# Gated linear attention in a two-block transformer kernel: values' products of two chunks in one, an empty state left out, keys masked by ScalarE, a low-rank gate on four column groups

## Chip, cores and metric

One NeuronCore of a Trainium2 chip runs the whole kernel. The metric is the device time of one execution in microseconds (us), as the median over runs. Everything is float32.

## What is computed

Two blocks over 256 tokens of width 1024. The first block has two layers. Layer 0 mixes tokens with a delta rule and a sparse attention; layer 1 mixes them with gated linear attention (the "second mixer", which the change touches); each layer ends in a mixture of 32 experts. The second block (two more layers) is not touched. The second mixer, cut to what matters:

```python
def gla_mixer(h, w_in, w_gate2, b_gate2, out_norm, w_out):
    q, k, v, r, glr = split_cols(h @ w_in, [512, 512, 1024, 1024, 16])
    log_a = log_sigmoid(glr @ w_gate2 + b_gate2) / 16          # low-rank gate, rank 16
    o = gla_chunked(heads(q), heads(k), heads(v), heads(log_a))  # 4 heads, chunks of 64 tokens
    o = rms_norm(o, out_norm) * silu(heads(r))
    return o @ w_out

def step(state, xs):                       # one chunk of one head; state starts as zeros
    q_i, k_i, v_i, b_i = xs                # b_i: running sum of log_a in the chunk
    bl = b_i[-1:]
    o_inter = (q_i * exp(b_i)) @ state
    att = causal(sum_d q_i k_i exp(b_i - b_j))
    o = o_inter + att @ v_i
    state = state * exp(bl).T + (k_i * exp(bl - b_i)).T @ v_i
    return state, o
```

## The kernel before

All engines' programs are written out by hand and meet at semaphores (`q.e.wait_ge`, `.then_inc`); each engine runs its own list in order. Weights come through a ring of six slots of 2 MB in SBUF. SyncE (SP) issues one transfer per slot, in a fixed order, and waits only for `unit_done`, the count of pieces of work ("units") with which TensorE has let go of a slot (line 337 outside the experts, line 355 in their loop). PSUM has eight banks of 512 floats per partition.

The second mixer on TensorE is `pe_gla`, in this order:

- `pe_gla_in`: as soon as the normalised input arrives (eight pieces, ScalarE line 494), line 1480 makes the 16 gate features from eight products of 128x16 weights with 256 tokens. Then two slots of query and key features (helper `pe_features`, line 432), with the gate's second product (line 1489) between them, and two slots of values (helper `accumulate`, line 400). Queries and keys are laid out by feature, values by token.
- `pe_gla_att`: for two token tiles (t) and four heads, the 64x64 products inside each chunk (line 1584) into bank 0, and the transposes of the decayed keys (line 1587) into banks 1 and 2.
- VectorE (`dve_gla_att`) then masks: for each of the two chunks of a tile (par) the scores (line 1594) and the keys (line 1595, the other chunk's tokens made zero), and clears the state `gS` (line 1596). Only then it signals `att_read`, for which TensorE waits.
- `pe_gla_scan`, for each of four chunks: the keys' product with the values, which is what is added to the state (line 1608); the state's product with the decayed queries (line 1614) and the values' product with the masked scores (line 1615), eight each, 64 columns wide, one pair for each half of a head's output; and then one "fill", eight products of the output gate `r` (`pe_gla_fill`, line 400), under which VectorE forms the next state (line 1626).
- `pe_gla_out`: sums of squares per head (line 1391), more fills, and `pe_out`, the product with `w_out` (line 696), followed by the router and the experts of layer 1 (lines 1920, 1944, 1953, 1967, 1902).

A float32 product is two instructions in the trace (two MATMUL and two LDWEIGHTS), so the x-counts of lines 1480, 1489, 1608, 1614 and 1615 are twice the number of products; the transposes are one instruction each.

Of the kernel before, what the change touches and what calls it, by code (L numbers as in the profile page):

```python
# [19 lines left out]
P = 128  # L20
D = 1024
KD = D // P
S = 256
# [103 lines left out]
def parameter_columns(a):  # L127
# [10 lines left out]
    c["gdn_norm"] = cols(a["gdn_out_norm"][0])  # L138
    c["gla_w2"] = pad(np.asarray(a["gla_w_gate2"][0]))
    c["gla_b2"] = cols(a["gla_b_gate2"][0])  # L140
# [56 lines left out]
dve_step act_step  # L197
inputs_in constants_in moment_ready glr_ready x_ready scaled_ready unit_done lin_read silu_c ada_copied ada_columns ada_read
sq_ready sum_ready rstd_ready norm_ready root_ready var_ready
# [17 lines left out]
def build(nc, a, vec_at, vec_w, dense_at, out):  # L217

    ctx = ExitStack()
    with ctx:  # L220
# [1247 lines left out]
        eq, ek, eb, ed = (view(A0 + 9472 + 1024 * j, H, S) for j in range(4))  # L1468
        att = view(A0 + 13568, 2, TH, CH)
        gkd = view(A0 + 14592, 2, TH, P)  # L1470
# [4 lines left out]
        def pe_gla_in(q):  # L1475
            u = Units(q)
            s = slot(q)
            for k in range(KD):
                q.e.wait_ge(sems["norm_ready"], q.due("norm_ready"))
                ins = mm(psum[0:16, 5, 0:S], narrow(s, 16)[:, k, :], hT[:, k, :], start=(k == 0), stop=(k == KD - 1))  # L1480
            ins.then_inc(sems["unit_done"], 1)
            for j in range(2):
                s = slot(q)
                for n in range(2):
                    pe_features(u, s, hT, 2 * P * n)
                if j == 0:
                    q.e.wait_ge(sems["glr_ready"], q.due("glr_ready"))
                    for h in range(H):
                        ins = mm(banks(6, 2, H, S)[:, h, :], v("gla_w2")[0:16, P * h:P * h + P], glr[0:16, :], start=True, stop=True)
                    ins.then_inc(sems["cums_ready"], 1)  # L1490
            for j in range(2):
                s = slot(q)
                for t in range(NT):
                    pe_tokens(u, s, hT, 0, 512, t)
            u.end()

        def act_gla_in(q):
            q.e.wait_ge(sems["unit_done"], q.due("unit_done"))
            A.activation(glr[0:16, :], psum[0:16, 5, 0:S], ACT.Copy).then_inc(sems["glr_ready"], 1)
            for j in range(2):  # L1500
# [75 lines left out]
        def pe_gla_att(q):  # L1576
# [11 lines left out]
            ins.then_inc(sems["att_ready"], 1)  # L1588

        def dve_gla_att(q):  # L1590
            q.e.wait_ge(sems["att_ready"], q.due("att_ready"))
            half = v("half", 2, CH)
            for par in range(2):
                V.tensor_tensor(att[:, par], banks(0, 1, TH, CH), over(half[:, par, :], TH), ALU.mult)
                V.tensor_scalar(gkd[:, par], banks(1, 2, TH, P), v("par")[:, par:par + 1], None, ALU.mult)
            V.memset(gS, 0.0).then_inc(sems["att_read"], 1)
            q.e.wait_ge(sems["att_read"], q.due("att_read"))

        def pe_gla_scan(q):

            q.e.wait_ge(sems["att_read"], q.due("att_read"))
            outs = banks(4, 4, 2 * H, S)
            for c in range(NCH):
                t, par = c // 2, c % 2
                if c > 0:
                    q.e.wait_ge(sems["state_ready"], q.due("state_ready"))
                for h in range(H):
                    ins = mm(psum[:, 2 + h // 2, S * (h % 2):S * (h % 2) + S], gkd[:, par, t * H + h, :], gv[:, t, S * h:S * h + S],
                             start=True, stop=True)
                ins.then_inc(sems["dstate_ready"], 1)  # L1610
                for h in range(H):
                    for i in range(2):
                        o = outs[:, 2 * h + i, CH * c:CH * c + CH]
                        mm(o, gS[:, h, P * i:P * i + P], eb[:, h, CH * c:CH * c + CH], start=True, stop=False, skip_group_check=True)
                        ins = mm(o, gv[:, t, S * h + P * i:S * h + P * i + P], att[:, par, t * H + h, :], start=False, stop=True,
                                 skip_group_check=True)
                ins.then_inc(sems["scan_out"], 1)
                pe_gla_fill(q, c)
            pe_gla_fill(q, NCH)

        def dve_gla_scan(q):
            for c in range(NCH - 1):
                q.e.wait_ge(sems["dstate_ready"], q.due("dstate_ready"))
                q.e.wait_ge(sems["scan_out"], q.due("scan_out"))
                for h in range(H):
                    ins = V.scalar_tensor_tensor(out=gS[:, h, :], in0=gS[:, h, :], scalar=ebl[:, NCH * h + c:NCH * h + c + 1],
                                                 in1=psum[:, 2 + h // 2, S * (h % 2):S * (h % 2) + S], op0=ALU.mult, op1=ALU.add)
                ins.then_inc(sems["state_ready"], 1)
            q.skip("dstate_ready")
            q.skip("scan_out")  # L1630
# [50 lines left out]
        def act_gla(q):  # L1681
            act_gla_in(q)
            act_gla_out(q)
            q.skip("unit_done", 4)
# [1290 lines left out]
```

## Time and profile before

| what | value |
|---|---|
| median of 3 runs | 2617.33 us (2615.58 to 2617.4) |
| the profiled execution's own time | 2615.79 us |
| its span | 2614.0 us |
| mean granted TensorE clock | 0.985 of full |
| second mixer, from its first product to its last product of `w_out`'s stage | 808.8 to about 966 us of the span |

The rows further down come from the profiled execution. Times in them are from the start of its span. PE is TensorE's matrix products, PEld its weight loads, DVE is VectorE, ACT is ScalarE, SPq is SyncE's queue. A granted clock of 1.00 is 2.4 GHz and 0.50 is 1.2 GHz.

### The profile page before, as it was taken

To read this page: it belongs to the slowest core of one execution; us is meant where nothing else is said; L and a number is where in the kernel's file an instruction comes from. 1 tells how busy PE (TensorE), PEld (TensorE's weight loads), DVE (VectorE), ACT (ScalarE), POOL (GpSimd) and SP (SyncE) were. 2 spreads that over 40 slices of the span, in tenths; PEclk is the share of its full clock that TensorE was granted. 3 is DMA by queue.
4 is the path that set the end of the run, shared out by engine and by line. 5 is a ranking of instruction groups with operands and counts; after the bars stand their busy time and mean duration, and the time that the engine had idled before them with its cause. 6 is when DMAs were issued, how large, how long until landed. Compare 5 with 4: busy or idle time off the path is not lost.

```text
span 2614.0 us, 28378 instructions
## 1 busy us (share of the span) xinstructions
PE 2441.6 (93%) x11488; PEld 1398.9 (54%) x11488; DVE 676.6 (26%) x1400; ACT 450.1 (17%) x814; POOL 0.2 (0%) x4
## 2 busy tenths in 40 slices
PE   7999999888889999988888999999999999999998
PEld 5775743333336673333333777774444777874443
DVE  3653321111003232101001533134112533042113
ACT  3141110000002121000000133102111242112111
POOL 0000000000000000000000000000000000000000
PEclk9999999999999999999999899999999999999999
DMA  9348669999997138999999532246999232148994
GB/s 402 132 188 366 250 282 428 428 429 428 428 427 289 73 129 335 429 428 428 429 428 427 215 129 97 97 192 239 425 422 416 110 129 97 65 193 331 426 421 187
DMA packets 53941, 769.64 MB, mean 294 GB/s; under 512 B 5984, under 2 KB 6496, under 8 KB 7008
## 3 DMA queue, kind: packets, MB, share of 16 engines
q1 hardware_dynamic: 53568, 768.17, 71.2%
q8 instruction: 62, 1.02, 0.1%
q10 hardware_dynamic: 288, 0.26, 0.1%
q14 instruction: 23, 0.19, 0.0%
HBM read 767.36 MB, written 1.05 MB: 294 GB/s over the span
## 4 chain that ended last, share of the span: by engine, by line
PE 71%; DMA 23%; DVE 3%; ACT 2%; issue 1%; SPq 0%; ACTq 0%; DVEq 0%
DMA slab<-in_experts 22%; PE psum L400 14%; PE psum L432 13%; PE psum L1930 8%; PE psum L1920 8%; PE psum L1967 7%; PE psum L1902 6%; PE psum L696 4%; PE psum L503 1%; DMA slab<-in_dense 1%; PE psum L1240 1%; PE psum L1953 1%; PE psum L626 0%; PE psum L1944 0%; PE psum L746 0%
## 5 line engine op out<-in xcount | busy, mean ns | idle before, releaser
L1920 PE MATMUL psum<-slab 128*64 128x512 f32 x2048 | 461.1, 597 | 77.6 <-DMA slab<-in_experts 73.8
L400 PE MATMUL psum<-slab 128*128 128x256 f32 (+6 forms) x1560 | 389.1, 406 | 12.2 <-ACT slab L2480 7.0
L1967 PE MATMUL psum<-slab 128*64 128x512 f32 x1536 | 359.5, 603 | 2.6 <-ACT slab L1998 2.6
L432 PE MATMUL psum<-slab 128*128 128x256 f32 x1504 | 345.4, 391 | 11.8 <-DVE slab L2770 6.6
L1920 PEld LDWEIGHTS psum<-slab 128*64 128x64 f32 x2048 | 142.1, 137 | 390.3 <-issue 274.7
L400 PEld LDWEIGHTS psum<-slab 128*128 128x128 f32 (+2 forms) x1560 | 272.9, 188 | 121.6 <-issue 70.6
L432 PEld LDWEIGHTS psum<-slab 128*128 128x128 f32 x1504 | 294.1, 196 | 60.9 <-issue 8.8
L1902 PE MATMUL psum<-slab 128*128 128x256 f32 x1024 | 249.3, 385 | 1.2 <-DVE slab L2020 1.2
L1930 PE MATMUL psum<-slab 128*64 128x512 f32 x1024 | 225.3, 592 | 0.0
L1902 PEld LDWEIGHTS psum<-slab 128*128 128x128 f32 x1024 | 183.2, 189 | 72.7 <-issue 50.3
L2010 DVE TENSOR_TENSOR slab<-psum,slab 128x512 f32<-128x512 f32 (+1 forms) x64 | 35.7, 558 | 691.6 <-PE psum L1920 502.3
L1967 PEld LDWEIGHTS psum<-slab 128*64 128x64 f32 x1536 | 99.3, 137 | 182.1 <-issue 178.5
L1930 PEld LDWEIGHTS psum<-slab 128*64 128x64 f32 x1024 | 73.4, 137 | 145.3 <-issue 145.0
L1994 ACT ACTIVATE slab<-psum 128x512 f32<-128x512 f32 (+1 forms) x64 | 31.4, 491 | 600.8 <-PE psum L1920 346.8
L696 PE MATMUL psum<-slab 128*128 128x256 f32 x512 | 114.8, 381 | 0.0
L696 PEld LDWEIGHTS psum<-slab 128*128 128x128 f32 x512 | 95.9, 189 | 17.0 <-issue 3.7
L2020 DVE COPY slab<-psum 128x256 f32<-128x256 f32 x64 | 27.2, 425 | 287.7 <-PE psum L1953 287.7
L1998 ACT ACTIVATE slab<-psum 128x512 f32<-128x512 f32 (+1 forms) x64 | 31.4, 491 | 387.0 <-PE psum L1944 387.0
L2026 DVE COPY slab<-psum 128x512 f32<-128x512 f32 x64 | 44.3, 692 | 147.0 <-PE psum L1967 147.0
L2002 ACT ACTIVATE slab<-psum 128x512 f32<-128x512 f32 x64 | 38.2, 597 | 198.6 <-PE psum L1967 198.6
L447 ACT ACTIVATE slab<-psum 128x512 f32<-128x512 f32 (+3 forms) x45 | 25.4, 565 | 243.3 <-PE psum L432 173.5
L2768 DVE TENSOR_TENSOR slab<-psum,slab 128x1024 f32<-128x1024 f32 x16 | 19.6, 1225 | 182.9 <-PE psum L400 182.9
(429 smaller groups left out, 1565.0 us busy)
## 6 DMA issues: line engine op xcount, KB each, us to landing
slab<-in_experts SPq DMA_DIRECT2D x288, 2048.0 KB, 20.2
slab<-in_dense SPq DMA_DIRECT2D x73, 2048.0 KB, 9.2
slab<-in_dense SPq DMA_DIRECT2D x2, 1680.0 KB, 16.8
slab<-in_vec SPq DMA_DIRECT2D x1, 2571.5 KB, 33.0
slab<-in_dense SPq DMA_DIRECT2D x1, 1328.0 KB, 27.6
slab<-in_dense SPq DMA_DIRECT2D x2, 640.0 KB, 13.9
slab<-in_xT SPq DMA_DIRECT2D x1, 1024.0 KB, 8.4
out<-slab SPq DMA_DIRECT2D x2, 512.0 KB, 2.6
```

The costliest lines, as they stand in the source:

```text
L400: ins = mm(out_ap, lhs, rhs, start=(n == 0), stop=(n == len(pairs) - 1), skip_group_check=True)
L432: ins = mm(psum[:, b, S * j:S * j + S], narrow(s, width)[:, k, c0 + P * j:c0 + P * j + P], src[:, k, :], start=(k == 0), stop=(k == KD - 1 ...
L696: ins = mm(psum[:, b, S * j:S * j + S], sl(w[n // 2], KD)[:, k, c0:c0 + P], src[:, k, :], start=(part is early and j == 0 and k == early[0 ...
L1902: ins = mm(y[:, c, :], ysl[:, P * c:P * c + P], gatedT, start=begin and c % 2 == 0, stop=False, skip_group_check=True)
L1920: ins = mm(psum[CAP * e:CAP * e + CAP, n, :], xg[:, k, CAP * e:CAP * e + CAP], sl(w, KD)[:, e * (KD // 2) + i, :], start=(k == 0), stop=(k ...
L1930: ins = mm(psum[CAP * e:CAP * e + CAP, 0, :], xg[:, k, CAP * e:CAP * e + CAP], sl(w[e], KD)[:, k, :], start=(k == 0), stop=(k == KD - 1), ...
L1967: ins = mm(psum[CAP * e:CAP * e + CAP, 2 + half, :], hidT[:, f, CAP * e:CAP * e + CAP], w, start=(f == 0), stop=(f == fc - 1), skip_group_ ...
L1994: A.activation(sil[:, 0:f], psum[:, 0, 0:f], ACT.Silu).then_inc(sems["silu_ready"], 1)
L1998: A.activation(hidT[:, 0:f // P, :], banks(0, 1, f // P, P), ACT.Copy).then_inc(sems["hidT_ready"], 1)
L2002: A.activation(ysl[:, 0:512], psum[:, 2, :], ACT.Copy).then_inc(sems["half_ready"], 1)
L2010: V.tensor_tensor(hid[:, 0:f], up, sil[:, 0:f], ALU.mult).then_inc(sems["hid_ready"], 1)
L2026: V.tensor_copy(ysl[:, 512:], psum[:, 3, :]).then_inc(sems["results_ready"], 1)
```

## The change

Five edits in the second mixer:

1. The gate features are made on four groups of 32 columns of TensorE: product k writes partitions 32(k mod 4) to 32(k mod 4)+31 of bank 5. The 128 rows then hold four partial sums, and the second product runs over all 128 rows, with `w_gate2` (16 rows, padded with zeros to 32) repeated four times, so that it adds them up.
2. The keys are masked by ScalarE (`act_gla_keys`, four activations of 512 columns with a scale per partition) while VectorE masks the scores alone, a tile at a time, with a signal after each tile.
3. The masked scores of a tile's two chunks stand beside each other, so that the values' product is made once for each tile, 128 columns wide.
4. Chunk 0 has no product with the empty state, the last chunk has no product of keys and values (nothing reads its state), and the state is not cleared: its first value is a copy.
5. Order in the scan: the values' products of tile 0 wait only for the first mask signal and run before the keys' products; the first fill waits for the second.

```diff
-    c["gla_w2"] = pad(np.asarray(a["gla_w_gate2"][0]))
+    c["gla_w2"] = np.concatenate([pad(np.asarray(a["gla_w_gate2"][0]))[:32]] * 4)
...
-        att = view(A0 + 13568, 2, TH, CH)
+        att = view(A0 + 13568, TH, P)
...
-                ins = mm(psum[0:16, 5, 0:S], narrow(s, 16)[:, k, :], hT[:, k, :], start=(k == 0), stop=(k == KD - 1))
+                g = k % 4
+                ins = mm(psum[32 * g:32 * g + 32, 5, 0:S], sl(s, KD)[:, 0, 16 * k:16 * k + 32], hT[:, k, :], start=(k < 4), stop=(k >= 4),
+                         skip_group_check=True)
...
-                        ins = mm(banks(6, 2, H, S)[:, h, :], v("gla_w2")[0:16, P * h:P * h + P], glr[0:16, :], start=True, stop=True)
+                        ins = mm(banks(6, 2, H, S)[:, h, :], v("gla_w2")[:, P * h:P * h + P], glr, start=True, stop=True)
...
-            A.activation(glr[0:16, :], psum[0:16, 5, 0:S], ACT.Copy).then_inc(sems["glr_ready"], 1)
+            A.activation(glr, psum[:, 5, 0:S], ACT.Copy).then_inc(sems["gla_copied"], 1)
...
+        def act_gla_keys(q):
+            q.e.wait_ge(sems["att_ready"], q.due("att_ready"))
+            for t in range(NT):
+                for par in range(2):
+                    ins = A.activation(gkd[:, par, t * H:t * H + H, :], banks(1 + t, 1, H, P), ACT.Copy, scale=v("par")[:, par:par + 1])
+            ins.then_inc(sems["gla_copied"], 1)
...
-            for par in range(2):
-                V.tensor_tensor(att[:, par], banks(0, 1, TH, CH), over(half[:, par, :], TH), ALU.mult)
-                V.tensor_scalar(gkd[:, par], banks(1, 2, TH, P), v("par")[:, par:par + 1], None, ALU.mult)
-            V.memset(gS, 0.0).then_inc(sems["att_read"], 1)
-            q.e.wait_ge(sems["att_read"], q.due("att_read"))
+            for t in range(NT):
+                own = slice(t * H, t * H + H)
+                for par in range(2):
+                    ins = V.tensor_tensor(att[:, own, CH * par:CH * par + CH], banks(0, 1, TH, CH)[:, own, :], over(half[:, par, :], H), ALU.mult)
+                ins.then_inc(sems["att_read"], 1)
...
-            q.e.wait_ge(sems["att_read"], q.due("att_read"))
             outs = banks(4, 4, 2 * H, S)
             for c in range(NCH):
                 t, par = c // 2, c % 2
+                if c == 0:
+                    q.e.wait_ge(sems["att_read"], q.due("att_read"))
+                if par == 0:
+                    for h in range(H):
+                        for i in range(2):
+                            ins = mm(outs[:, 2 * h + i, P * t:P * t + P], gv[:, t, S * h + P * i:S * h + P * i + P], att[:, t * H + h, :],
+                                     start=(c == 0 and i == 0), stop=False, skip_group_check=True)
+                if c == 0:
+                    ins.then_inc(sems["scan_out"], 1)
+                    q.e.wait_ge(sems["gla_copied"], q.due("gla_copied"))
+                else:
+                    q.e.wait_ge(sems["state_ready"], q.due("state_ready"))
+                if c < NCH - 1:
+                    for h in range(H):
+                        ins = mm(psum[:, 2 + h // 2, S * (h % 2):S * (h % 2) + S], gkd[:, par, t * H + h, :], gv[:, t, S * h:S * h + S],
+                                 start=True, stop=True)
+                    ins.then_inc(sems["dstate_ready"], 1)
                 if c > 0:
-                    q.e.wait_ge(sems["state_ready"], q.due("state_ready"))
-                for h in range(H):
-                    ins = mm(psum[:, 2 + h // 2, S * (h % 2):S * (h % 2) + S], gkd[:, par, t * H + h, :], gv[:, t, S * h:S * h + S],
-                             start=True, stop=True)
-                ins.then_inc(sems["dstate_ready"], 1)
-                for h in range(H):
-                    for i in range(2):
-                        o = outs[:, 2 * h + i, CH * c:CH * c + CH]
-                        mm(o, gS[:, h, P * i:P * i + P], eb[:, h, CH * c:CH * c + CH], start=True, stop=False, skip_group_check=True)
-                        ins = mm(o, gv[:, t, S * h + P * i:S * h + P * i + P], att[:, par, t * H + h, :], start=False, stop=True,
-                                 skip_group_check=True)
-                ins.then_inc(sems["scan_out"], 1)
+                    for h in range(H):
+                        for i in range(2):
+                            ins = mm(outs[:, 2 * h + i, CH * c:CH * c + CH], gS[:, h, P * i:P * i + P], eb[:, h, CH * c:CH * c + CH],
+                                     start=False, stop=(par == 1), skip_group_check=True)
+                    ins.then_inc(sems["scan_out"], 1)
+                if c == 0:
+                    q.e.wait_ge(sems["att_read"], q.due("att_read"))
                 pe_gla_fill(q, c)
             pe_gla_fill(q, NCH)
...
-                q.e.wait_ge(sems["scan_out"], q.due("scan_out"))
-                for h in range(H):
-                    ins = V.scalar_tensor_tensor(out=gS[:, h, :], in0=gS[:, h, :], scalar=ebl[:, NCH * h + c:NCH * h + c + 1],
-                                                 in1=psum[:, 2 + h // 2, S * (h % 2):S * (h % 2) + S], op0=ALU.mult, op1=ALU.add)
-                ins.then_inc(sems["state_ready"], 1)
-            q.skip("dstate_ready")
+                if c == 0:
+                    q.skip("scan_out")
+                    V.tensor_copy(gS, banks(2, 2, H, S)).then_inc(sems["state_ready"], 1)
+                    q.e.wait_ge(sems["state_ready"], q.due("state_ready"))
+                else:
+                    q.e.wait_ge(sems["scan_out"], q.due("scan_out"))
+                    for h in range(H):
+                        ins = V.scalar_tensor_tensor(out=gS[:, h, :], in0=gS[:, h, :], scalar=ebl[:, NCH * h + c:NCH * h + c + 1],
+                                                     in1=psum[:, 2 + h // 2, S * (h % 2):S * (h % 2) + S], op0=ALU.mult, op1=ALU.add)
+                    ins.then_inc(sems["state_ready"], 1)
+                    q.e.wait_ge(sems["state_ready"], q.due("state_ready"))
             q.skip("scan_out")
...
         def act_gla(q):
             act_gla_in(q)
+            act_gla_keys(q)
             act_gla_out(q)
```

## Rows read from the trace of the kernel before

**Rows 1.** The page's chain that ended last, share of the span by engine.

```profile
PE 71%; DMA 23%; DVE 3%; ACT 2%; issue 1%; SPq 0%; ACTq 0%; DVEq 0%
```

**Rows 2.** The DMA queue's waits, 790 to 1200: us in total, times, longest us.

```profile
SPq L355 <- PE psum L1920: 117.5, 32, 16.4
SPq L337 <- PE psum L400: 88.3, 4, 45.1
```

**Rows 3.** Windows by stage: busy us of PE, PEld, DVE, ACT, POOL; clock, DMA share, GB/s.

```profile
808.70:814.05 5.35, 5.24 (x16) 1.87 (x16) 2.17 (x6) 2.76 (x7) 0.00 (x0) 0.68 1.00 423
1100.00:1500.00 400.00, 357.73 (x1613) 161.28 (x1612) 71.89 (x161) 35.13 (x58) 0.00 (x0) 0.98 0.94 396
```

**Rows 4.** Timeline of the mixer's first stage: start us, us, engine, line.

```profile
808.16 3.30 ACT L494 ACTIVATE slab<-slab 128x256 f32<-128x256 f32 x8 [1.59 <-DVE slab L2142]
808.82 5.31 PE L1480 MATMUL psum<-slab 128*16 128x256 f32 x16 [1.27 <-ACT slab L494]
810.69 0.15 PEld L1480 LDWEIGHTS psum<-slab 128*16 128x16 f32 x1 [0.28 <-ACT slab L494]
811.12 0.15 PEld L1480 LDWEIGHTS psum<-slab 128*16 128x16 f32 x1 [0.28 <-issue]
814.05 14.14 PE L432 MATMUL psum<-slab 128*128 128x256 f32 x64
```

**Rows 5.** Timeline: 32-column groups after a full product, and what follows them.

```profile
920.44 1.08 PE L1391 MATMUL psum<-slab 128*32 128x256 f32 x16
921.44 3.74 PE L400 MATMUL psum<-slab 128*128 128x256 f32 x16
```

**Rows 6.** Timeline from the scores to the scan's first product.

```profile
873.41 1.09 PE L1587 MATMUL psum<-slab 128*128 128x128 f32 x8
874.54 0.69 DVE L1594 TENSOR_TENSOR slab<-psum,slab 128x512 f32<-128x512 f32 x1 [12.74 <-PE psum L1587]
878.38 0.91 DVE L1596 MEMSET slab<- 128x1024 f32 x1 [0.16 <-issue]
879.34 3.78 PE L1608 MATMUL psum<-slab 128*128 128x256 f32 x8 [4.83 <-DVE slab L1596]
```

**Rows 7.** Windows of 0.5 us at the clock's steps, columns as in rows 3.

```profile
812.50:813.00 0.50, 0.50 (x4) 0.23 (x3) 0.00 (x0) 0.00 (x0) 0.00 (x0) 1.00 1.07 459
877.50:878.00 0.50, 0.00 (x0) 0.00 (x0) 0.50 (x1) 0.00 (x0) 0.00 (x0) 0.50 1.05 426
884.50:885.00 0.50, 0.50 (x7) 0.50 (x6) 0.00 (x0) 0.00 (x0) 0.00 (x0) 1.00 0.00 0
```

**Rows 8.** Timeline of the scan: chunk 1 from its keys' product, and chunk 3's end.

```profile
882.92 0.52 PE L1614 MATMUL psum<-slab 128*128 128x64 f32 x2
887.03 3.69 PE L400 MATMUL psum<-slab 128*128 128x256 f32 x16
890.56 1.90 PE L1608 MATMUL psum<-slab 128*128 128x256 f32 x8
892.29 0.33 PE L1614 MATMUL psum<-slab 128*128 128x64 f32 x2
895.81 3.69 PE L400 MATMUL psum<-slab 128*128 128x256 f32 x16
896.08 1.66 DVE L1626 SCALAR_TENSOR_TENSOR slab<-slab,psum 128x256 f32<-128x256 f32 x4 [7.08 <-PE psum L1615]
913.35 7.16 PE L400 MATMUL psum<-slab 128*128 128x256 f32 x32
```

**Rows 9.** Timeline: products 128 columns wide with 128x128 weights.

```profile
974.55 3.84 PE L400 MATMUL psum<-slab 128*128 128x128 f32 x32 [0.84 <-DVE slab L1798]
```

**Rows 10.** Timeline: ScalarE's four activations with operands per partition, 512 columns.

```profile
969.31 2.79 ACT L678 ACTIVATE slab<-psum,slab 128x512 f32<-128x512 f32 x4 [0.23 <-DVE slab L657]
```

**Rows 11.** Groups of VectorE by form: busy us, mean ns, idle before.

```profile
L2010 DVE TENSOR_TENSOR slab<-psum,slab 128x256 f32<-128x256 f32 x32 | 13.6, 424 | 189.3 <-ACT slab L1994 189.3
L2694 DVE COPY slab<-psum 128x1024 f32<-128x1024 f32 x2 | 2.4, 1224 | 19.1 <-PE psum L2676 19.1
```

More of the change, by code:

```diff
@@ L197 @@
 dve_step act_step
-inputs_in constants_in moment_ready glr_ready x_ready scaled_ready unit_done lin_read silu_c ada_copied ada_columns ada_read
+inputs_in constants_in moment_ready gla_copied x_ready scaled_ready unit_done lin_read silu_c ada_copied ada_columns ada_read
 sq_ready sum_ready rstd_ready norm_ready root_ready var_ready
@@ L1486, in pe_gla_in @@
                 if j == 0:
-                    q.e.wait_ge(sems["glr_ready"], q.due("glr_ready"))
+                    q.e.wait_ge(sems["gla_copied"], q.due("gla_copied"))
                     for h in range(H):
-                        ins = mm(banks(6, 2, H, S)[:, h, :], v("gla_w2")[0:16, P * h:P * h + P], glr[0:16, :], start=True, stop=True)
+                        ins = mm(banks(6, 2, H, S)[:, h, :], v("gla_w2")[:, P * h:P * h + P], glr, start=True, stop=True)
                     ins.then_inc(sems["cums_ready"], 1)
@@ new lines, in pe_gla_scan @@
+                if c == 0:
+                    ins.then_inc(sems["scan_out"], 1)
+                    q.e.wait_ge(sems["gla_copied"], q.due("gla_copied"))
+                else:
[5 more added lines that the diff above has]
+                    ins.then_inc(sems["dstate_ready"], 1)
```

## The prediction

> **What bounds the kernel now.** I read the chain that ended last first: 71% of it is TensorE and 23% transfers, VectorE and ScalarE have 5% between them [rows 1]. So a microsecond counts where TensorE is the one that is waited for, and for the transfers one must ask what starts them. The DMA queue's waits answer that: in the experts' loop (line 355) and outside it (line 337) SyncE waits for TensorE's units, and for nothing that runs by a clock of its own [rows 2]. In the experts of layer 1 the transfers are the pace (DMA share 0.94, TensorE 358 of 400 us busy, not 400) [rows 3], but their stream begins when the first slots are let go, which is when the mixer has ended. So whatever the mixer loses or gains on TensorE moves the start of that stream, and all that comes later, by the same amount: I take the factor as 1. In the mixer's first stage the transfers are at 1.00 of their time [rows 3], but TensorE passes from the gate features into the next slot's work without a gap [rows 4], so the weights were there.
>
> Inside the mixer the timeline shows TensorE as the chain nearly throughout, with one real hole: from the end of the transposes to the scan it waits 4.83 us for VectorE's masks [rows 6]. The windows show two stretches at half the granted clock (1.2 GHz): one before 812.5 us in the first stage, whose mean clock is 0.68 [rows 3, 7], and one from about 877 us, in that hole, to about 884 us [rows 7].
>
> **Term 1, gate features on column groups.** Before: the 16 instructions of line 1480 start at 808.82 and line 432 follows at 814.05. The inputs came earlier: ScalarE's eighth piece ends at 808.16 + 3.30 = 811.46. What made the end late is that at 1.2 GHz one instruction takes 0.43 us (811.12 - 810.69) while a piece needs two and arrives every 0.41 [rows 4]. On four groups products of different groups overlap: the sixteen 32-column instructions of line 1391 take 921.44 - 920.44 = 1.00 us, against the 3.5 us that sixteen full ones of the same length take (887.03 to 890.56) [rows 5, 8]. Then TensorE keeps up, and only the last piece's own two instructions lie behind its arrival: 811.46 + 0.05 for the signal (879.34 after VectorE's 878.38 + 0.91 [rows 6]) + 2 x 0.43, and 0.1 for the change back to full width (four rounds of 0.215 are 0.86, and line 1391 took 1.00), is 812.45. Gain 814.05 - 812.45 = 1.6. Bounds: 1.9 if the clock were back by then; 0.2 if it had never been low, since at 0.215 us an instruction the old order keeps up with the pieces too. I take 1.6, for nothing ahead of it changes. Wider weights (32 columns for 16), the second product over 128 rows for 16 and the copy over 128 partitions cost nothing: eight instructions of 256 columns take 1.90 with all 128 rows too [rows 8], and the copy has those 14 us of line 432's work over it [rows 4].
>
> **Term 2, the masks.** Before: transposes end, VectorE starts at 874.54, runs 4.8 us, TensorE starts at 879.34 [rows 6]. After: VectorE's first signal comes after two TENSOR_TENSORs of 256 columns at 0.42 [rows 11], overlapping a little: 0.8 us. TensorE starts at 875.4. Gain 3.95. The second signal is due 0.8 later and is wanted only by the first fill, 3.5 us later; nothing stands there. ScalarE's four activations start at 874.54 too. The nearest row has two operands per partition and takes 2.79 for four [rows 10]; the new ones have one, so 2.4 to 2.8, ready at 876.9 to 877.4. ScalarE had nothing to do then (its next work is the first fill's output), and it reads banks 1 and 2, VectorE bank 0. TensorE wants the keys when the values' products of tile 0 are done, at 875.4 + 1.8 = 877.2. Stall 0 to 0.25; I take 0.1. If ScalarE were twice as slow, 2.8.
>
> **Term 3, fewer products.** Sixteen products (eight with the state, eight with the values) take 895.81 - 892.29 = 3.52 us, 0.22 each, 0.11 an instruction [rows 8]. Now merge two chunks: is a 128-column product dearer than a 64-column one? Thirty-two instructions of just that form take 978.39 - 974.55, that is 3.84 us with their start, 0.12 each [rows 9]. The weight load sets both, so the merged product costs what one of the two did, and half of 32 are gone, and eight of 32 state products with chunk 0: 24 x 0.22 = 5.3. [...] Lower bound from the rows: 0.12 for 0.11, 0.3 us less. Chunk 3's keys' products: eight instructions, 892.29 - 890.56 = 1.73 [rows 8]. Nobody reads them. Gain 1.73. Together 7.0.
>
> **Term 4, the state.** VectorE forms the state under a fill: 1.66 us, begun 0.27 after the fill begins, against 3.5 of fill [rows 8]. The first state is now a copy of 1024 columns, 1.22 [rows 11], begun after the keys' products, also under the fill. Cost 0 with 1.6 us to spare; without the fill it would be 1.9 for a state and 1.5 for the copy. The clearing (0.91) was in the hole of term 2 and is counted there.
>
> **Term 5, the clock in the scan.** The low stretch begins in the hole and ends in chunk 0. Chunk 0's keys' products took 882.92 - 879.34 = 3.58 against 1.73, its sixteen others 887.03 - 882.92 = 4.11 against 3.52 [rows 6, 8]: 1.85 + 0.59 = 2.4. With the hole down to 0.9 us I expect the clock to stay at 2.4 GHz. Gain 2.4; bounds 0 (it falls all the same) and 2.4.
>
> **The rest.** Everything from the last state products on (squares, two fills, roots, `w_out`) keeps its order and its distances. Check by a walk, in the old times: 875.4, tile 0's values 1.8, stall 0.1, keys 1.73, fill 3.5: 882.5; chunk 1 1.73 + 1.76 + 3.5: 889.5; chunk 2 8.8: 898.3; chunk 3 1.76: 900.1. Before, the fills after chunk 3 begin at 913.35 [rows 8]. That is 13.2, and 1.6 of term 1 makes **14.8 us**.
>
> **How the numbers follow.** The profiled execution took 2615.79; 2615.79 - 14.8 = 2601.0. The median of the runs is 1.5 us higher, so the median after should be 2617.33 - 14.8 = **2602.5**. The bound of no change is 0.2%, 5.2 us, for all that follows.
>
> **Rivals.**
> - *The clock falls after all.* TensorE still pauses for 0.9 us after the transposes. Against it: it fell some 3 us into a hole of 4.83 us [rows 6, 7], and this one is over sooner. Price 1.7 to 2.4: 2604.2 to 2604.9. 12%. The Trainium skill (TensorE: Matmul & The Clock Gate, Part 4) holds that transposes don't count as work for the clock gate, which would make this likelier; no row here separates them.
> - *The column groups give nothing*, because the pieces are the pace or the low stretch lies elsewhere: term 1 is 0.2, 2603.9. 6%.
> - *A 128-column product costs two.* 3.5 back: 2606.0. Against it rows 9. 6%.
> - *The gain doesn't reach the end*, because the experts' transfers run on a schedule that the mixer doesn't set: 2617. Against it, every wait of SyncE is for TensorE [rows 2]. 5%.
> - *Slower: TensorE stays at 1.2 GHz through the scan.* Its products are now mostly short ones behind weight loads; if those don't bring the clock up, the 24.7 us of work from 875.4 to 900.1 take 49.4. That gives back 24.7 of 14.8, and ends 9.9 above before: 2627.2. Half of the low time is lost, so it decides from 29.6 us at the low level. Against it: the clock rose at 884 us in the middle of just such products [rows 7]. 2%.
> - The forecast itself: 69%.
>
> Faster by over 0.2% in the first three rivals and the forecast: 0.93. Same 0.05, slower 0.02. Range: the forecast's own terms run from 14.2 to 15.5 (2601.8 to 2603.1); the three small rivals reach 2606.0; the runs of before spread over 1.8 us. So 2600.0 to 2606.5.
>
> **What would show it.** Line 1480's last product ends about 1 us after ScalarE's last piece. TensorE's hole before the scan is under 1 us and the granted clock there 1.00. The values' products, 32 instructions in two runs of 16, take 1.8 us a run. No stall over 0.3 before the first keys' products; none before the state's. Seven fills as before. The experts' first transfers shift by 14 to 15 us. The prediction is wrong if the stretch from the last norm piece to `w_out` is not 14 to 15 us shorter, or if it is and the end isn't.

## The result, and the profile after

| | before | changed |
|---|---|---|
| median | 2615.31 us (6 runs, 2612.49 to 2617.4) | 2600.06 us (6 runs, 2599.09 to 2604.06) |
| profiled execution, its own time | 2615.79 us | 2600.23 us |
| its span | 2614.0 us | 2598.6 us |

The ratio is 0.994 with an interval of 0.9928 to 0.9952, a gain of 15.3 us between the medians. In a second comparison on another occasion (5 and 9 runs) it was 0.9941 (0.9928 to 0.9955). The forecast was a gain of 14.8 us and a median of 2602.5.

The page's chain by engine is the same line as in [rows 1], and SyncE still waits for TensorE only. Its first transfer in the experts' loop (line 355) is issued at 968.90 where it was 982.17, 13.3 us sooner, in an execution whose mixer began 2.2 us later. Its longest wait outside that loop was 45.1 us and is 31.6 now, because the units it waits for in the scan come sooner (the waits of [rows 2]):

```profile
SPq L337 <- PE psum L400: 74.9, 4, 31.6
```

The first stage, from the timeline (the counterpart of [rows 4]); line 1481 is the gate features' product now, line 1491 the gate's second product:

```profile
810.37 3.31 ACT L494 ACTIVATE slab<-slab 128x256 f32<-128x256 f32 x8 [1.59 <-DVE slab L2168]
811.02 3.67 PE L1481 MATMUL psum<-slab 128*32 128x256 f32 x16 [1.27 <-ACT slab L494]
814.62 14.13 PE L432 MATMUL psum<-slab 128*128 128x256 f32 x64
828.59 1.89 PE L1491 MATMUL psum<-slab 128*128 128x256 f32 x8
830.32 14.03 PE L432 MATMUL psum<-slab 128*128 128x256 f32 x64
844.18 27.63 PE L400 MATMUL psum<-slab 128*128 128x512 f32 x64
```

TensorE now follows ScalarE's pieces: they end at 813.68, and line 432 starts 0.94 later (before, 2.59 later). First gate product to line 432 is 3.60 us, before 5.23. The same part of the timeline before, from the gate's second product (line 1489) on:

```profile
828.12 1.99 PE L1489 MATMUL psum<-slab 16*128 16x256 f32 x8
844.01 27.63 PE L400 MATMUL psum<-slab 128*128 128x512 f32 x64
```

From the first query and key product to the first values' product (line 400) it was 844.01 - 814.05 = 29.96 us and is 844.18 - 814.62 = 29.56 now. The windows show that the gate features of the changed kernel were made at 1.2 GHz too (columns as in [rows 3]):

```profile
811.00:814.62 3.62, 3.60 (x17) 1.42 (x17) 2.08 (x6) 2.68 (x7) 0.00 (x0) 0.53 1.02 430
814.62:816.00 1.38, 1.38 (x7) 1.24 (x7) 0.00 (x0) 0.38 (x1) 0.00 (x0) 1.00 1.10 427
```

From the scores to the scan and through it (the counterpart of [rows 6] and [rows 8]); line 1586 is the scores, 1605 VectorE's masks, 1596 ScalarE's, 1618 the values' products, 1627 the keys', 1633 the state's, 1646 the copy of the first state, 1651 the later states:

```profile
873.58 1.09 PE L1589 MATMUL psum<-slab 128*128 128x128 f32 x8
874.71 1.42 DVE L1605 TENSOR_TENSOR slab<-psum,slab 128x256 f32<-128x256 f32 x4 [12.74 <-PE psum L1589]
874.71 2.42 ACT L1596 ACTIVATE slab<-psum,slab 128x512 f32<-128x512 f32 x4 [2.27 <-PE psum L1589]
875.52 2.05 PE L1618 MATMUL psum<-slab 128*128 128x128 f32 x16 [0.85 <-DVE slab L1605]
877.41 1.90 PE L1627 MATMUL psum<-slab 128*128 128x256 f32 x8
879.15 3.63 PE L400 MATMUL psum<-slab 128*128 128x256 f32 x16
879.35 1.22 DVE L1646 COPY slab<-psum 128x1024 f32<-128x1024 f32 x1 [3.22 <-PE psum L1627]
882.61 1.90 PE L1627 MATMUL psum<-slab 128*128 128x256 f32 x8
884.35 1.89 PE L1633 MATMUL psum<-slab 128*128 128x64 f32 x16
886.08 3.69 PE L400 MATMUL psum<-slab 128*128 128x256 f32 x16
...
900.11 7.15 PE L400 MATMUL psum<-slab 128*128 128x256 f32 x32
```

The hole before the scan is 0.85 us where it was 4.83. ScalarE is done at 877.13, VectorE with all scores at 876.13, and TensorE comes for the keys at 877.3: no stall worth naming. Every later product begins where the one before it ends. And the clock stayed up from the scores to the scan's end:

```profile
873.00:901.00 28.00, 27.15 (x188) 24.78 (x183) 5.95 (x13) 4.99 (x7) 0.00 (x0) 1.00 0.18 71
```

**The walk.** The figure that I follow through the experiments is the *stretch*, from the first product of the gate features to the first product with `w_out` (line 696), both read from the timeline; what is left of the span is the *rest*, in which all kernels here but the last two have the same code.

| kernel | stretch begins | stretch | rest |
|---|---|---|---|
| before | 808.8 | 124.9 | 2489.1 |
| changed | 811.0 | 109.4 | 2489.2 |
| changed, once more | 810.7 | 109.7 | 2489.4 |
| old gate chain | 814.1 | 111.5 | 2493.9 |
| before, column groups alone | 812.4 | 122.4 | 2487.5 |
| gate chain at full width | 808.4 | 110.9 | 2488.6 |
| values' products 64 wide | 808.5 | 113.0 | 2481.1 |
| keys masked by VectorE | 810.1 | 110.7 | 2487.3 |
| all masks first | 809.5 | 113.8 | 2485.9 |
| hole filled with products | 810.0 | 113.2 | 2486.1 |
| hole filled with transposes | 811.4 | 112.5 | 2490.0 |
| scores early | 808.3 | 107.6 | 2488.6 |
| scores early, fillers at layer 0's end | 808.5 | 107.2 | 2485.3 |
| scores early, fillers at four ends | 808.7 | 107.2 | 2484.8 |

The stretch lost 15.5 us and the rest nothing (2489.1, 2489.2). That these two rests agree so closely is in part luck, for the rests of the other kernels, with the same code there, lie between 2481.1 and 2493.9. That what the mixer gained reaches the end whole rests on the medians: 15.3 us here and 16.1 in the second comparison, for 15.5 in the stretch.

### The profile page after: what moved, and what is told of

It is laid out like the page before. It is cut to its first block, busy times and chain, and to the rows that moved or that the text cites. A ratio compares the mean times of both kernels' runs of the same rounds, so it can differ in the third digit from the quotient of the medians.

```text
span 2598.6 us, 28266 instructions
## 1 busy us (share of the span) xinstructions
PE 2428.8 (93%) x11432; PEld 1390.5 (54%) x11432; DVE 672.8 (26%) x1396; ACT 452.2 (17%) x818; POOL 0.2 (0%) x4
## 4 chain that ended last, share of the span: by engine, by line
PE 71%; DMA 23%; DVE 3%; ACT 2%; issue 1%; SPq 0%; ACTq 0%; DVEq 0%
DMA slab<-in_experts 22%; PE psum L400 14%; PE psum L432 13%; PE psum L1956 8%; PE psum L1946 8%; PE psum L1993 7%; PE psum L1928 6%; PE psum L696 4%; PE psum L503 1%; DMA slab<-in_dense 1%; PE psum L1240 1%; PE psum L1979 1%; PE psum L626 0%; PE psum L1970 0%; PE psum L746 0%
```

## The experiments

**Old gate chain.** The changed kernel with the first edit undone.

```diff
-                ins = mm(psum[32 * g:32 * g + 32, 5, 0:S], sl(s, KD)[:, 0, 16 * k:16 * k + 32], hT[:, k, :], start=(k < 4), stop=(k >= 4),
+                ins = mm(psum[0:16, 5, 0:S], narrow(s, 16)[:, k, :], hT[:, k, :], start=(k == 0), stop=(k == KD - 1))
...
+                        ins = mm(banks(6, 2, H, S)[:, h, :], v("gla_w2")[0:16, P * h:P * h + P], glr[0:16, :], start=True, stop=True)
```

> The changed kernel with the gate features made by the old chain of 16 columns. Measure: the stretch from the first gate-feature product to the first product with w_out, 109.4 us in the changed kernel, 124.9 in the one before. By terms: 1.6 of the chain comes back, and 0.3 for which the walk has no term yet, seen around the gate's second product (16 rows before, 128 after): 111.3. Rival, the column groups give only what the late clock gives: where the clock is at 2.4 GHz during the chain, the stretch stays within 0.5 us of 109.4.

Measured: stretch 111.5, 2607.05 us for one execution. The chain:

```profile
814.07 5.33 PE L1480 MATMUL psum<-slab 128*16 128x256 f32 x16 [1.28 <-ACT slab L494]
819.33 13.92 PE L432 MATMUL psum<-slab 128*128 128x256 f32 x63
```

5.26 us to line 432, not 3.60, and the distance between the two query and key slots 15.99, not 15.70; from the first of them to the values' products it is 29.96, not 29.56. The terms hold; the clock was low here, so the rival was not tried at its own condition.

**Column groups alone**, on the kernel before.

> The kernel before with the column groups alone. By terms: the stretch is 124.9 - 1.9 = 123.0, with the hole before the scan still 4.8 us long and the granted clock low from inside the hole into the first chunk. Rival: products that fill only 32 columns each don't bring the clock back as fast as the chain did, and the query products after them run at 1.2 GHz for some us: 124 or more.

Measured: stretch 122.4, 2611.57 us for one execution. The hole is still 4.84 us, as the timeline has it:

```profile
881.12 3.65 PE L1610 MATMUL psum<-slab 128*128 128x256 f32 x8 [4.84 <-DVE slab L1598]
```

The windows show that the clock fell only just behind it and was low for 3.4 us. In the profile of before it fell inside the hole and was still low for 4.8 us of work behind it [rows 7]:

```profile
881.40:884.50 3.10, 3.10 (x8) 2.42 (x8) 0.00 (x0) 0.00 (x0) 0.00 (x0) 0.50 0.00 0
884.80:886.00 1.20, 1.20 (x13) 1.20 (x13) 0.00 (x0) 0.00 (x0) 0.00 (x0) 1.00 0.00 0
```

From the keys' first product to the end of chunk 3 it is 33.35 us here and 34.01 before: 0.66 of the 2.4 gained against forecast is the place of the fall. With it put back the stretch is 123.1 for 123.0 expected. In this execution the clock was low until 816.4, 0.35 us into the query products, and the rival's price, 124 or more, did not come. Among all profiles here in which the clock was low over the gate features, it rose 2.6 to 4.8 us after their first product with the groups, and 3.3 to 3.7 us after it with the three chains. So whether the groups ever delay it is not settled.

**Gate chain at full width**: 128 columns of weights, of which 16 count; the others meet rows of zeros.

```diff
+                ins = mm(psum[:, 5, 0:S], sl(s, KD)[:, 0, 16 * k:16 * k + 128], hT[:, k, :], start=(k == 0), stop=(k == KD - 1))
```

> The changed kernel with one chain of full width (128 columns of weights, of which 16 are the gate's, the others meet rows of zeros in the second product) and the second product over 128 rows. If the 0.3 us at the second product comes from its 16 rows, this kernel keeps that gain and loses only the overlap of groups: 109.4 + 1.6 = 111.0, and the distance from the first to the second slot of query and key products is 15.7, not 16.0. Rival, the 0.3 belongs to the column groups: 111.3 and 16.0.

The timeline (line 1480 the gate features, 1489 the second product):

```profile
808.44 5.32 PE L1480 MATMUL psum<-slab 128*128 128x256 f32 x16 [1.27 <-ACT slab L494]
813.59 14.03 PE L432 MATMUL psum<-slab 128*128 128x256 f32 x64
827.46 1.89 PE L1489 MATMUL psum<-slab 128*128 128x256 f32 x8
829.18 14.03 PE L432 MATMUL psum<-slab 128*128 128x256 f32 x64
```

Measured: stretch 110.9, 2601.18 us for one execution; first gate product to line 432 5.15, and 15.59 between the slots. So the gain at the second product doesn't belong to the column groups: it comes from its 128 rows, with which there is no step between row widths on either side of it. This kernel is another 0.1 below the changed one's 15.70 because it has no step back from narrow weights either: its first slot takes 13.87 us, behind the groups it takes 13.97.

**Values' products 64 wide.**

```diff
-                            ins = mm(outs[:, 2 * h + i, P * t:P * t + P], gv[...], att[:, t * H + h, :], ...)
+                            for x in range(2):
+                                ins = mm(outs[:, 2 * h + i, P * t + CH * x:P * t + CH * x + CH], gv[...],
+                                         att[:, t * H + h, CH * x:CH * x + CH], ...)
```

> The changed kernel with each values' product of 128 columns split into two of 64 with the same weights. By terms a product of either width costs 0.22, so 16 more cost 3.5 us: the stretch is 112.9. Rival, a product's time goes by its columns: no change, 109.4.

The timeline of the values' products (line 1619) and the keys' (1629):

```profile
873.00 3.79 PE L1619 MATMUL psum<-slab 128*128 128x64 f32 x32 [0.85 <-DVE slab L1605]
876.62 1.96 PE L1629 MATMUL psum<-slab 128*128 128x256 f32 x8
```

Measured: 3.62 us for 32 instructions where the changed kernel has 1.89 for 16 of twice the width; stretch 113.0. An instruction of 64 or of 128 columns with its weight load costs 0.11 us. This execution took 2595.77 us, less than the changed kernel, with a stretch 3.6 longer: its rest was 8.1 shorter. One execution's total says nothing about a few microseconds here.

**Keys masked by VectorE**, after the scores, as before the change.

```diff
+            for par in range(2):
+                ins = V.tensor_scalar(gkd[:, par], banks(1, 2, TH, P), v("par")[:, par:par + 1], None, ALU.mult)
+            ins.then_inc(sems["gla_copied"], 1)
...
-            act_gla_keys(q)
```

> The changed kernel with the keys masked by VectorE, after the scores. TensorE still starts with the values' products 0.8 us after the transposes, but the keys are ready only after 1.4 + 2.5 us of VectorE, at 3.95 after the transposes, when the values' products have been done for 1.3 us: stretch 109.4 + 1.4 = 110.8, clock at 2.4 GHz throughout the scan. Rival, ScalarE's help is worth the whole of the old wait: 113 or more.

The timeline: values' products (line 1621), VectorE's masking of the keys (1608), keys' products (1630):

```profile
874.61 2.05 PE L1621 MATMUL psum<-slab 128*128 128x128 f32 x16 [0.85 <-DVE slab L1605]
875.13 2.46 DVE L1608 TENSOR_SCALAR slab<-psum,slab 128x1024 f32<-128x1024 f32 x2
877.65 2.00 PE L1630 MATMUL psum<-slab 128*128 128x256 f32 x8 [0.99 <-DVE slab L1608]
```

Measured: 3.04 us from the values' products to the keys', for 1.89, and stretch 110.7; 2600.69 us, ratio 0.9943 (0.9927 to 0.9958) beside 0.9941 for the changed kernel in the same comparison. ScalarE's part is worth 1.2 us; the rest of the hole went because the values' products no longer wait for the keys.

**All masks first**: the same, and the scan waits for them all.

```diff
                 if c == 0:
                     q.e.wait_ge(sems["att_read"], q.due("att_read"))
+                    q.e.wait_ge(sems["gla_copied"], q.due("gla_copied"))
```

> As e4, and the scan begins only when all masks are done: a hole of about 4 us before the scan, as before the change (4.8), with all other edits in. By terms: 3.1 us of the hole come back, and the clock falls inside it, which costs 1.7 to 2.4 more: stretch 114.2 to 114.9. Rival, the clock doesn't go by the hole: 112.5 with 2.4 GHz throughout. Total time between the two kernels, 5 us above the changed one.

The timeline, with the values' products in line 1622 and the keys' in 1630:

```profile
876.75 3.59 PE L1622 MATMUL psum<-slab 128*128 128x128 f32 x16 [3.98 <-DVE slab L1608]
880.13 2.01 PE L1630 MATMUL psum<-slab 128*128 128x256 f32 x8
```

The windows in the hole and after it:

```profile
873.00:876.50 3.50, 0.00 (x0) 0.00 (x0) 3.50 (x6) 0.00 (x0) 0.00 (x0) 1.00 1.02 435
877.00:880.00 3.00, 3.00 (x16) 3.00 (x16) 0.00 (x0) 0.00 (x0) 0.00 (x0) 0.50 0.02 5
```

Measured: stretch 113.8, 2604.31 us, ratio 0.9956 (0.9941 to 0.9971). The hole is 3.1 longer and the clock is low right behind it: the 16 values' instructions take 3.38 for 1.89. From the last transpose to `w_out` it is 50.76 us, 46.02 in the changed kernel: 3.13 of hole and 1.6 of clock. The clock was expected to fall inside the hole; it fell some 0.2 us behind its end and was low for 3.4 us of work. The stretch is 0.4 under the range expected (114.2 to 114.9): the clock cost a little less than 1.7, and in this execution the gate features took 3.25 us for 3.60, because the clock rose sooner there. The total was 3.5 above the changed kernel's, not 5. The hole itself is 0.85 shorter than before the change, with the clearing of the state gone from it.

**The hole filled.** The kernel just shown, with work in the hole that nothing reads: eight products of 256 columns, or 32 transposes.

```diff
+                    for _ in range(8):
+                        mm(psum[:, 3, 0:S], ident, v("gla_w2")[:, 0:S], start=True, stop=True)
```

> As the kernel in which the scan waits for all masks (hole 4.25 us from the last transpose to the scan's first product, clock low from inside it), with eight products of 256 columns into a free bank, 3.4 us of work that nothing reads, put into the hole. If the clock falls because TensorE stands still, it stays at 2.4 GHz here and the stretch is 113.8 - 1.6 = 112.2. Rival, the clock falls by something else in this place: again 113.8.

> The same, with 32 transposes (0.11 us each, 3.5 us) in the hole instead of the products. If transposes keep the clock up as products do, the stretch is 112.2 to 112.4. Rival, by which transposes don't count: the clock is low as in the kernel with the bare hole and the stretch 113.8 or, as more of it lies in the scan, up to 114.5.

The timeline with products in the hole (line 1618; 1624 the values', 1632 the keys'):

```profile
874.14 3.62 PE L1618 MATMUL psum<-slab 128*128 128x256 f32 x16
878.28 2.02 PE L1624 MATMUL psum<-slab 128*128 128x128 f32 x16 [0.52 <-DVE slab L1608]
880.14 1.90 PE L1632 MATMUL psum<-slab 128*128 128x256 f32 x8
```

The same with transposes in the hole (line 1618):

```profile
874.83 3.65 PE L1618 MATMUL psum<-slab 128*128 128x128 f32 x32
878.98 2.02 PE L1624 MATMUL psum<-slab 128*128 128x128 f32 x16 [0.49 <-DVE slab L1608]
```

The clock after the hole with transposes:

```profile
877.00:880.00 3.00, 2.51 (x23) 2.30 (x22) 1.83 (x2) 0.00 (x0) 0.00 (x0) 1.00 0.62 257
```

Measured: from the last transpose of the keys to `w_out` 49.12 and 49.14 us, for 50.76 with the bare hole. The scan begins just as late (4.25 us) and at 2.4 GHz. The clock fell in or just behind the hole in all three profiles with a bare hole of about 4 us and more, and in neither of these two, one execution each (2600.95 us with products, 2604.21 with transposes). So it is TensorE's standing still that brings the clock down, worth 1.6 us, and transposes hold it as well as products. The stretch was 112.5 with transposes, as expected, and 113.2 with products, a miss by 1: there the clock was low over the gate features for 6.8 us and into the query products (16.23 us between the slots for 15.70), ahead of the place in question.

**The changed kernel once more.**

> The changed kernel once more, unchanged, to see what moves between executions. By the walk the stretch from the first gate-feature product to the first w_out product is again 109.4 within 0.5, unless the clock's low stretch lies otherwise; outside it the two executions differ by several us at places where TensorE pauses, by where the granted clock falls. Rival, the difference between kernels outside the mixer (-7.6 and +5 us) belongs to the change: it is there again, at the same places.

Measured: 2600.78 us (2598.3 to 2602.47, 5 runs), stretch 109.7. The differences outside the mixer were partly there again and partly not. The windows over 1510 to 1660 us, first before (mean clock 0.97):

```profile
1510.00:1660.00 150.00, 139.43 (x644) 109.62 (x643) 53.05 (x53) 48.11 (x85) 0.00 (x0) 0.97 0.30 109
```

then the changed kernel (1.00):

```profile
1510.00:1660.00 150.00, 139.44 (x694) 116.12 (x692) 51.57 (x48) 46.67 (x86) 0.00 (x0) 1.00 0.30 107
```

and the changed kernel once more (0.97):

```profile
1510.00:1660.00 150.00, 139.44 (x671) 115.18 (x670) 51.53 (x48) 46.16 (x84) 0.00 (x0) 0.97 0.29 104
```

The same program has 1.00 in one execution and 0.97 in the next over 150 us. Over 2000 to 2250 us it is the other way round: 0.97 before, 0.95 in the changed kernel, 0.97 in the changed kernel once more. So a clock that falls at one layer's end and not at another's needs no change of the program; these places are not to be put down to the change.

**Scores early.** The hole and the pause ahead of the scores are both covered by the last piece of the values' products: scores, transposes and masks go ahead of it, and the wait for its copy goes behind the first values' products, which don't need it. The transposes wait until ScalarE has read bank 2 (`need`).

```diff
                 for t in range(NT):
+                    if j == 1 and t == 1:
+                        pe_gla_att(q, u)
                     pe_tokens(u, s, hT, 0, 512, t)
-            u.end()
...
+            u.need(u.n)
...
+                if n == 3:
+                    act_gla_keys(q)
...
                     q.e.wait_ge(sems["gla_copied"], q.due("gla_copied"))
+                    q.last_units.end()
```

> The changed kernel with the score products and transposes moved ahead of the last piece of the values' products, the keys' masking ahead of that piece's copy, and the wait for that copy behind the values' products of tile 0. Both pauses of TensorE (0.7 us before the scores, 0.85 before the scan) go: stretch 109.4 - 1.5 = 107.9, total 1.5 us below the changed kernel. Rival, the pauses move: the transposes wait for ScalarE to read bank 2 (up to 0.3), and what waits at the scan is the last copy: stretch 109 or more.

The timeline from the transposes (line 1594) over the last piece of values (400) to the scan (1623 the values' products, 1633 the keys'); ScalarE masks in line 1601:

```profile
863.30 1.09 PE L1594 MATMUL psum<-slab 128*128 128x128 f32 x8
864.23 7.03 PE L400 MATMUL psum<-slab 128*128 128x512 f32 x16
864.43 2.42 ACT L1601 ACTIVATE slab<-psum,slab 128x512 f32<-128x512 f32 x4 [1.51 <-PE psum L1594]
871.10 1.95 PE L1623 MATMUL psum<-slab 128*128 128x128 f32 x16
872.88 1.90 PE L1633 MATMUL psum<-slab 128*128 128x256 f32 x8
```

Measured: stretch 107.6, no pause left between 863 and the scan's end; 2597.13 us (5 runs, 2595.82 to 2597.91), ratio 0.9926 (0.9912 to 0.9939), against 2600.78 for the changed kernel in the same comparison. The slowest of its five executions is faster than the fastest of those five. The stretch is 0.3 shorter than expected: 1.76 from the two pauses, and the stall of 0.1 on the keys went too. The walk gives 1.8 us of the 3.7 between these two medians; the rest I can't tell from the spread.

**Fillers at layer 0's end.** On top of the scores early, products that nothing reads in the two pauses ahead of the gate features: five ahead of the wait for the statistics' scales, three after the products that spread them.

```diff
+            if m == 0:
+                for _ in range(5):
+                    mm(psum[:, 5, 0:S], ident, v("gla_w2")[:, 0:S], start=True, stop=True)
```

> The kernel with the scores early (stretch 107.6 us), with five and three products that nothing reads in the two pauses ahead of the gate features, where TensorE waits for the statistics and the first normalised piece. If the low stretch over the gate features comes from these pauses, the clock is 2.4 GHz there, and the last piece's two instructions take 0.43 instead of 0.86: 3.2 from the first gate product to the first query product instead of 3.6, stretch 107.1. Rival, the pauses are too long to be covered and the clock falls all the same: 107.6.

Windows over the pauses and the gate features, with the fillers:

```profile
803.50:808.50 5.00, 4.78 (x24) 3.71 (x25) 4.24 (x16) 0.93 (x3) 0.00 (x0) 1.00 1.00 423
808.50:812.00 3.50, 3.50 (x18) 1.32 (x18) 2.08 (x6) 2.79 (x8) 0.00 (x0) 1.00 1.01 431
```

and in the kernel with the scores early alone:

```profile
803.50:808.30 4.80, 1.29 (x8) 0.86 (x8) 4.03 (x15) 0.92 (x3) 0.00 (x0) 1.00 0.99 423
808.30:812.00 3.70, 3.67 (x17) 1.45 (x17) 2.09 (x6) 2.68 (x7) 0.00 (x0) 0.54 1.02 434
```

Measured: the clock is 1.00 over the gate features instead of 0.54, they take 3.24 us instead of 3.62, and the stretch is 107.2. In all twelve profiles without fillers the clock was low over the gate features, and in neither of the two with them. One execution, 2594.22 us.

**Fillers at four ends**, the same after each mixture of experts.

> The same fillers after each of the four expert mixtures, on top of the scores early. If the low stretches there are worth what half the clock costs, the total is 1 to 4 us below that of the scores early (2597.1 beside 2616.9), and the executions spread less. Rival, TensorE is not what is waited for in these places, or the fillers delay the rows' products: same total or 0.5 us more.

Measured: 2594.07 us (6 runs, 2592.39 to 2598.35), ratio 0.9918 (0.9902 to 0.9935), mean granted clock 0.991 where the scores early had 0.987. The median is 3.1 us below that of the scores early, which was taken in another comparison, and the two intervals overlap; that the fillers gain outside the mixer is likely and not shown. The executions spread over 6.0 us, more than the 2.1 of the scores early, so that part of the expectation was wrong.

## Where the prediction held, and the step that failed

The mechanisms of the five terms came as forecast, and the median lies inside the range, by 0.06 us. By its own sign the prediction failed: it called itself wrong if the stretch was not 14 to 15 us shorter, and the stretch is 15.5 shorter. The step that failed is a term put at nothing. Of "the second product over 128 rows for 16" the prediction says that it costs nothing; it counted no gain for it, and the change of rows gained 0.4 us.

*Term 1, 1.6 us.* Measured 5.23 - 3.60 = 1.63. The overlap is what it rests on: full width without groups gave 5.15. The allowance of 0.1 for the step back to full width holds where the clock is 1.00 (fillers at layer 0's end): line 432 starts 0.60 us behind the last piece there, of which the signal and two instructions are 0.48. In the changed kernel it was 0.94 for 1.01 expected, with the clock rising in the last 0.2 us. (The prediction's own sum gives 812.47 and not 812.45.) That the same is worth only 0.2 at 2.4 GHz was not tried.

*The term that was missing, 0.4.* I compared the second product over 128 rows with a product over 128 rows elsewhere (1.90 us), and never asked what the 16 rows of before had cost. From the first query and key product to the values' products it is 29.96 us before and with the old chain, and 29.56 in the changed kernel. The 0.4 lie in the second product (1.92 to 1.73 from start to start), in the slot ahead of it (0.1) and in the slot behind it (0.1). The 128 rows cost nothing, as the prediction said; what it missed is that the 16 rows had cost something, at the change of rows on both sides of the old product.

*Term 2, 3.95.* Measured 4.83 - 0.85 = 3.98. Of this 0.85 is the clearing of the state, which is gone (the hole is 3.98 with all masks first); 2.0 is the order, values before keys; and 1.2 is ScalarE's help, as the kernel without it shows. The prediction did not split it.

*The stall on the keys, 0.1.* The keys' products follow 1.89 us after the values' first, of which 1.78 are the products when nothing stands behind them: 0.1.

*Term 3, 7.0.* The products 64 wide cost 3.6 us more, against 3.5 expected: between 64 and 128 columns this kernel doesn't pay by columns. Leaving out chunk 0's state products and chunk 3's keys' products was not tried by itself; the timeline shows them gone, at 1.73 us each for such a run. From the scan's start to the fills after chunk 3 it is 24.59 us, for 24.7 in the walk.

*Term 4, 0.* The copy began 0.2 us into the fill and was over 2 us before its end.

*Term 5, 2.4.* The clock stayed up. Its price was read from the profile of before and is not a constant: it is half of the low time that TensorE works in. That was 4.8 us before (2.4), and 3.4 with the groups alone (1.7) and with all masks first (1.6), where the clock fell only behind the hole and the whole low time was shorter, 3.4 us for 6.8. One profile could not say which of the two is typical of the kernel before.

*Factor 1.* The rest is 2489.1 before and 2489.2 after; the medians, 15.3 and 16.1, bear the factor out within the spread. The fills that the prediction counts as seven are eight in both traces, and nothing hangs on it.

So the stretch gained 15.5 where the walk said 14.8: 0.4 from the missing term, 0.1 from the scan's walk, and less than 0.2 from roundings. *The level was the other weak step.* I gave executions a spread of 1.8 us, from three runs that lay close together and high. The eleven runs of the last comparison of the kernel before go from 2611.45 to 2623.49, and its median in the first comparison came out 2.0 below the three that I had. The median of the changed kernel, 2600.06, lies at the very edge of the range (2600.0) for that reason: the gain was 0.5 more than forecast and the level 2.0 lower. A range for the time should have reached some 3 us further down.

*The rivals.* The clock did not fall again; the groups gave their 1.6; a wide product cost what a narrow one does; the gain reached the end; the clock was up through the scan. Thirty-two transposes held 2.4 GHz through a hole behind which it otherwise fell. The Trainium skill (TensorE: Matmul & The Clock Gate, Part 4) says that transposes don't count as busy in the same way for the clock gate; for these float32 transposes the measurement decides against it (1.00 from 877 to 880 us).

## What to carry to other kernels

When an engine waits for several masks or copies, first ask which product needs which of them; putting the product that needs the least first was worth more here (2.0 us of hole) than a second engine's help (1.2). With 128x128 float32 weights a product of 64 columns costs as much as one of 128, so pair narrow ones that share weights. And follow a change through a stretch between two fixed instructions: here one execution with 3.6 us more work in it was 4.5 us faster in total.

## What the runs showed of the hardware

- A hole of 4 to 4.8 us on TensorE costs more than itself: 3.4 to 4.8 us of work at 1.2 GHz followed it, which is 1.6 to 2.4 us lost, and twice the clock fell only when the hole had just ended. Work that nothing reads, products or transposes alike, took that away (one execution each).
- Eight instructions over 16 rows between products over 128 rows cost 0.4 us more than the same eight over 128 rows (29.96 us against 29.56 from the slot ahead to the end of the slot behind). Behind narrow weights a full-width slot takes 0.1 us more (13.97 against 13.87).
- Sixteen instructions on four groups of 32 columns overlap though the two of one product go to the same group: at 1.2 GHz they kept pace with pieces that came every 0.40 us, where the chain, at 0.43 an instruction, needed 0.86 for each [rows 4].
- The time outside the mixer varied from 2481.1 to 2493.9 us among executions with the same code there.
